# Sample attention: the DMAs of the V pages issued from ScalarE's queue in place of GpSimd's

## The reference, cut to what matters

```python
def one(args):                       # lax.map over the 8 samples
    pt, qi, ki, vi = args
    kp = cache_k[pt].reshape(past, N_ATT_HEADS, 2, ATT_HEAD_DIM)   # 32 pages x 128 x 512 floats
    vp = cache_v[pt].reshape(past, N_ATT_HEADS, ATT_V_DIM)         # 32 pages x 128 x 512 floats
    kf = concatenate([kp, ki]);  vf = concatenate([vp, vi])
    return _diff_attention(qi[None], kf[None], vf[None], q_pos, k_pos, rel_bias, lam)[0]
# _diff_attention: two softmaxes per head (q1 k1^T, q2 k2^T, with a T5 bias), w = p1 - lam*p2, then w @ v
```

## Time and profile before

| | before |
|---|---|
| median of 3 runs | 4429.04 us |
| profiled execution, own time | 4432.87 us |
| its span | 4431.2 us |
| mean granted PE clock over the span | 0.889 of full speed |
| DVE line 1070 in the first and last of seven looped bodies | 840.57 and 1185.05 us |
| last matmul of the stage (line 932) | starts at 1228.77 us |

### The profile page before, as it was taken

The page is one execution under the profiler, slowest core; times in us unless marked ns, Lnnn a source line. Parts: engine busy times, 40 slices in busy tenths (PEclk is TensorE's granted clock), DMA queues, the critical chain, the costliest instruction groups (busy, mean ns, idle before and its releaser), DMA issues. The chain is left out here.

```text
span 4431.2 us, 48459 instructions
## 1 busy us (share of the span) xinstructions
PE 3462.9 (78%) x12230; PEld 1663.3 (38%) x12230; DVE 2442.9 (55%) x5891; ACT 1350.9 (30%) x3845; POOL 1495.7 (34%) x1599
## 2 busy tenths in 40 slices
PE   5999665777766578687887888888878878788786
PEld 4446344544422233233333333333333333333332
DVE  1102354333245475857756855854864864874785
ACT  0110132333200233333333333343343333333333
POOL 0000000222300233444543544454443554454454
PEclk7999777888788889898999899899889899999989
DMA  8121603787734598998998998998998999999898
GB/s 330 47 46 29 22 1 104 273 287 281 262 142 144 226 376 311 379 387 355 421 396 340 418 399 329 416 420 335 417 410 330 398 416 376 380 421 375 363 418 344
DMA packets 245916, 1342.83 MB, mean 303 GB/s; under 512 B 47321, under 2 KB 60858, under 8 KB 94149
## 3 DMA queue, kind: packets, MB, share of 16 engines
q0 software_dynamic: 164352, 1174.49, 65.9%
q1 hardware_dynamic: 63456, 144.12, 10.6%
q10 hardware_dynamic: 17892, 21.83, 1.5%
HBM read 1319.30 MB, written 20.97 MB: 302 GB/s over the span
## 5 line engine op out<-in xcount | busy, mean ns | idle before, releaser
L1502 PE MATMUL psum<-sb_ring,sb_diag 128*128 128x512 f32 x4224 | 2089.9, 650 | 573.7 <-PEq L62 567.1
L1633 DVE CUSTOM_DVE_ANT_0 sb_ring<-sb_ring,sb_h_tiles 128x1024 f32<-128x1024 f32 x1056 | 1269.0, 1224 | 840.6 <-DMA sb_ring<-in_uv,sb_index_stage 808.7
L1502 PEld LDWEIGHTS psum<-sb_ring,sb_diag 128*128 128x128 f32 x4224 | 853.1, 208 | 1791.5 <-issue 1791.0
L1476 POOL DMA_INDIRECT sb_ring<-in_uv,sb_index_stage x1056 | 1256.5, 1190 | 628.6 <-POOLq L62 334.5
L1575 ACT ACTIVATE sb_gelu<-sb_dots 128x1 f32<-128x1 f32 x1056 | 210.9, 200 | 1153.9 <-ACTq L62 1136.6
L804 POOL DMA_DIRECT2D sb_v_pages<-in_cache_v x256 | 135.1, 528 | 1086.1 <-POOLq L62 1063.8
L1474 POOL COPY sb_index_stage<-sb_experts 128x4 uint32 (+1 forms) x264 | 93.7, 355 | 1052.5 <-POOLq L62 1050.5
L1580 ACT ACTIVATE sb_diag<-sb_ident,sb_expert_w 128x128 f32<-128x128 f32 x1024 | 411.1, 401 | 33.3
L1577 ACT ACTIVATE sb_expert_w<-sb_gelu,sb_gates 128x1 f32<-128x1 f32 x1056 | 311.0, 295 | 114.4 <-ACT sb_gelu L1575 3.8
L1520 PE MATMUL psum<-sb_w_pq,sb_h2T 128*128 128x512 f32 x576 | 259.3, 598 | 1.3 <-PEq L62 1.3
L866 PE MATMUL psum<-sb_ident,sb_k_pages 128*128 128x128 f32 x1024 | 153.3, 316 | 52.9 <-PEq L62 52.8
(11 more groups left out here) (212 smaller groups left out, 2459.2 us busy)
## 6 DMA issues: line engine op xcount, KB each, us to landing
sb_v_pages<-in_cache_v POOLq DMA_DIRECT2D x256, 256.0 KB, 4.4
sb_k_pages<-in_cache_k SPq DMA_DIRECT2D x256, 256.0 KB, 4.1
sb_w_ada<-in_w_ada SPq DMA_DIRECT2D x12, 2048.0 KB, 17.5
sb_ring<-in_uv,sb_index_stage POOLq DMA_INDIRECT x1056
sb_w_pq<-in_w_pq SPq DMA_DIRECT2D x4, 2048.0 KB, 17.1
sb_w_qkv<-in_w_in SPq DMA_DIRECT2D x3, 2048.0 KB, 19.4
sb_w_bcu<-in_w_in SPq DMA_DIRECT2D x12, 512.0 KB, 5.6
sb_h_tiles<-h_scratch SPq DMA_DIRECT2D x9, 512.0 KB, 8.0
```

Of the source, the lines that this page charges most:

```text
L1476: pool.indirect_dma_start(ring[:, slot, :], None, uv, bass.IndirectOffsetOnAxis(ap=stage[:, c % 4, s:s + 1], axis=0))\
L1502: ins = nc.tensor.matmul(psum[:, n, :], diag[:, slot, :], ring[:, slot, D + n * BANK:D + (n + 1) * BANK], start=(c == 0 and s == 0), stop= ...
L1633: dot = nc.vector.tensor_tensor_reduce(ring[:, slot, 0:D], ring[:, slot, 0:D], h2[:, u], 1.0, 0.0, ALU.mult, ALU.add, dots[:, slot:slot + 1])
```

## The change

POOL's block in sample_attention goes. ACT issues the same loads: in every body that has a `prev`, `load(act, cache_v, vp, "v", prev, c)` stands at the head of chunk c, behind `copy_keys(0)` and ahead of `copy_keys(c + 1)`.

```diff
-            @block.gpsimd
-            def _(pool):
-                pool.wait_ge(T["tab"], 16)
-                cache_v = A["cache_v"][0].rearrange("g p h d -> g p (h d)")
-
-                def body(b, prev):
-                    for c in range(NCH):
-                        if prev is not None:
-                            load(pool, cache_v, vp, "v", prev, c)
-                samples(pool, body)
-
...
             @block.scalar
             def _(act):
                 step = Steps(act, act_c)
+                act.wait_ge(T["tab"], 16)
+                cache_v = A["cache_v"][0].rearrange("g p h d -> g p (h d)")
                 act.wait_ge(T["setup"], 1)
...
                     if b is not None:
                         copy_keys(0)
                     for c in range(NCH):
+                        if prev is not None:
+                            load(act, cache_v, vp, "v", prev, c)
                         if b is not None and c + 1 < NCH:
                             copy_keys(c + 1)
```

## The result

The kernel after takes 4596.27 us (median of 4 runs, 4580.98 to 4603.88) against 4431.80 us for the kernel before in the same comparison: the ratio is 1.0365, with a 95% interval from 1.0323 to 1.0408. The prediction was 4616 us, in a range from 4525 to 4725.

What follows compares the result with a forecast made beforehand. Loads and transfers, at some 5 us a chunk in the dense part, were taken to set the pace. +181 us in seven bodies and +6 us in the last took 4433 to 4620, less 4: 4616 us, range 4525 to 4725.

Steps and rivals of the forecast that it cites:

- The pace: Looped bodies: PE falls into ACT's step; a chunk costs 8.3 us without and 9.8 with exp, against some 5.
- the order of waits: Behind ACT's load: the next key copy and the score copy wait, so PE's next scores and values wait too.
- The price of a load: ACT's queue: four register reads, a wait and four issues cost 5.4 us a load, as on SP.
- What is hidden: ACT's idle time in a body: 13 to 14 us cover a third of the loads' 43.2 us.
- The turn: Between samples: ACT stands 9.8 us where it stood 14.7, as part of the load hides there.
- The sum: Whole stage: a body 83.2 us against 57.4, +181 us in seven, +6 us in the last, together +187 us.
- The clock: PE in the stage, granted clock 0.81: PE may get less; the effect was taken as 0.
- No change: ACT's idle time takes the loads, which needs a load under 1.8 us: 4429 us, chance 0.04.
- Faster: Body ends and last body: V arrives sooner by ACT's queue, 54 us go: 4375 us, chance 0.05.
- Half the price: ACT's register reads take no time on the path, a load is 2.7 us: 4458 us, chance 0.11.
- SP and ACT hinder each other: ACT's issues wait out SP's, 1.9 us more a load: +120 us, 4736 us; chance 0.14, shared with slow register reads.

Runs made afterwards that it cites:

- e2: The kernel before (POOL loads V), with ACT also reading the four page numbers of every chunk and not using them: 4454.58 us, ratio 1.0062.
- e10: The kernel before (POOL loads V), with ACT also reading two page numbers a chunk and not using them: 4436.87 us, ratio 1.0011.
- e3: The kernel after with ACT loading V from fixed pages, so four issues a chunk and no register reads: 4467.90 us, ratio 1.0080.
- e6: As e3 (V from fixed pages by ACT), with K's loads moved from SP to POOL: 4470.47 us, ratio 1.0093.
- e5: The kernel after with a chunk's four page numbers read by one instruction, on SP and ACT: 4526.27 us, ratio 1.0195.
- e9: The kernel before (POOL loads V), with ACT also reading eight page numbers a chunk and not using them: 4544.69 us, ratio 1.0240.

## Why the prediction was right, point by point

**The pace.** Right. ACT's queue took the pace from SP's and POOL's, and PE now waits ahead of the scores, as the order of waits had it; the chunk is 7.86 us without exp, where 8.3 was predicted, and ACT's loads stand 7.8 to 9.8 us apart inside a body, where 8.3 to 9.8 was.

**The price of a load.** Nearly right: 5.21 us on the mean against 5.4. This is 8 x 0.19 = 1.5 us of the 2.8 between 83.2 and 80.4; the rest is in the handshakes, 16 of them 0.33 in place of 0.36 us (0.5) and the others shorter too. ACT reads (0.277 us) and issues (0.489) near SP's prices (0.264 and 0.473). The reads were measured alone: 2.70 - 0.33 = 2.37 us in e2, leaving 2.7 for the wait and the issues. A read with its register operations is thus 2.37 / 4 = 0.59 us, of which the TENSOR_LOAD itself is 0.277. The Trainium skill ("DMA: Bandwidth & Descriptors", section "Latency and other measured facts") gives a floor of some 600 ns for a `tensor_load`; the trace agrees for the whole read, not for the instruction alone.

**What is hidden.** Right as far as it was measured: a cover of 1.8 us a chunk was worked out, and e10 with 1.2 us shows nothing that can be told from 0 while e2 with 2.4 us does.

**The turn.** Right: 9.3 us of idle time on the mean of six turns and 0.5 us more before the second copy, 9.8 predicted. V landed sooner (3.5 us in the median against the 4.4 I used), and `values(7)` to the next key copy took the same 7.4 us, from 933.54 here, in the timeline of PE in the profile after, to 940.96 above:

```profile
933.54 1.90 PE L889 MATMUL psum<-sb_v_pages,sb_probsT 128*8 128x128 f32 x32 [2.37 <-PEq L62]
```

**The sum.** +187 us predicted, +164.5 between the medians, +147.9 in the profiled executions (that of the kernel after, 4580.98 us, is the fastest of its four). Of the 39 us between 187 and 148, the seven bodies have about 22, the last body 3.4 (it lost 2.6 and not 6), and 14 lie outside what the change touches (4.1 ahead of the stage, 1.5 in its first body, 8.1 behind it), which the spread of runs covers.

**The clock.** It fell, from 0.85 to 0.80 over six bodies, and PE's busy time for the same matmuls rose from 265 to 298 us. Taking 0 for it was right in effect: half of ACT's gaps stayed at 5.39 to 5.42 us, with no room for a wait for PE in them. In the others and at the turn a small part of the clock is not excluded.

**The rivals.** "No change" fails by e2 and e3, each of which costs more than nothing with half of a load. The rule of the Trainium skill behind it ("DMA: Bandwidth & Descriptors", section "Issuing engines are not separate DMA queues"), that the time to initiate is usually small beside the DMA, does not hold here, where five us of queue stand beside a landing time of 3.5. "Faster" fails on the same point; V did land sooner and PE waited less for it, but ACT set the pace. "Half the price" was refuted by the 5.40 us gaps and by e2, where reads alone take 2.37 us. "SP and ACT hinder each other" is refuted in the form it had by e6 and by the issues of e3 that overlap SP's.

## What to carry to other kernels

A DMA moved to a compute engine's queue costs that engine the register reads, address work, wait and issue of every transfer, in order with its compute, and none of it is counted as busy: add it up from the queue's rows and compare it with the engine's idle time chunk by chunk, less handshakes and less the idle time at the turns, not with its busy share. What fits under that cover cost next to nothing here, what exceeds it comes about once per chunk. In this kernel, reading several page numbers by one instruction (0.7%) and filling the turn between samples (1.1%) gained, where moving all or half of the V loads to ACT lost.

## What the runs showed of the hardware that I had not expected

- Issues of 256 KB DMAs that follow each other on ACT's queue end 0.646 us apart, whether register operations stand between them (the kernel after, where an issue shows as 0.489 us) or not (e3 and e6, where all but the first of four show as 0.616 to 0.617 us). Time the block of four, not the single issue.
- The transfers of V landed in 3.5 us in the median from ACT's queue in the kernel after, in 4.4 us from the same queue in e3 and from POOL's in the kernel before, and in 3.8 us both from ACT's queue in e5 and from POOL's in e9. Bodies are 80, 65, 57, 72 and 73 us long there: the landing time goes with how dense the loads are, and the queue makes no difference that shows.
- One reading instruction for four page numbers saved ACT about 1.0 us a load, not the 1.4 that three reads at full price would have been.
